# Input of the projection normalised for its later tiles, sample states read before their outer product is added

## The chip, the cores and the metric

The kernel runs on one core of a Trainium2 chip. The metric is the device time of one execution in microseconds (us). A core has TensorE (PE), VectorE (DVE), ScalarE (ACT), GpSimd (POOL) and SyncE (SP, which issues DMAs); each works through its own instructions strictly in order, and they wait for one another by semaphores.

## What is computed

Two layers of a hybrid decoder, on 256 prompt tokens and 8 samples side by side (264 columns). Cut to what matters here:

```
def decoder_layer(x, ...):
    x = x + 0.5 * swiglu(rmsnorm(x, norm_ffn1), ffn1_w_in, ffn1_w_out)
    h = rmsnorm(x, norm_mix)
    proj = h @ w_in
    p_rwkv, p_sc, p_ssm = jnp.split(proj, [RWKV_PROJ, RWKV_PROJ + SC_PROJ], axis=-1)
    ...                                   # three mixers, then w_out, then a second swiglu

rwkv7_mix:       xs = proj + (prev - proj) * mu          # prev: proj shifted by one token
short_conv_mix:  b_gate, c_gate, xt = jnp.split(proj, 3, axis=-1)
                 conv, new_buf = causal_depthwise_conv(c_gate * xt, buf, conv_w)
                 return rmsnorm(b_gate * conv, norm_g), new_buf
mamba2_mix, for a sample (one step):
                 h = h0 * exp(dt * A) + B (outer) (x * dt)
                 y = sum_n(C * h) + D * x
```

## The kernel before

A layer is a front stage and a back stage (`front_stage`, `back_stages`, called through `mix_stages`). The change lies in the front stage alone. There the first feed-forward runs (68 weight tiles), then the combined projection `h @ w_in`, 51 tiles of 128 output columns; tile n = 0 is the tail, 1 to 8 are xbc, 9 and 10 rwkv, 11 to 14 z, 15 to 18 x, 19 to 22 c, 23 to 26 b, 27 to 50 rwkv.

Each tile is 8 x 3 matmuls (`Stream.product`, L232 to L234): the fp32 weights are split into hi and lo, and so is the input. ScalarE makes hi (L209), VectorE or for some tiles GpSimd makes lo (L216). GpSimd makes lo for tiles 0, 2, 14, 16, 18, 20, 22, 24, 44 and 46. The product goes to one of three PSUM banks. The input of the projection is `x * gain` without the factor 1/rms: `norm2` makes `h_hi` and `h_lo` while the feed-forward ends, and the 1/rms (`rs`) is multiplied onto each product when VectorE evicts it (L1153 for rwkv tiles, L1159 for the others). TensorE may begin tile n when tile n-3 has been evicted.

For a rwkv tile VectorE evicts into `front_prev`; ScalarE then writes `mix.xs` (L1122) and `last` (L1124); VectorE adds the shifted part (`shift`, L1132).

Around the tiles, each engine has a side program (`side`) cut by `yield slot`: when the engine has come to tile n it runs the parts with slot <= n. The order of the work is thus written out by hand. VectorE, for tile n: evict(n), shift of tile n-1, lo of tile n+3, side steps. ScalarE, for tile n: side steps, hi of tile n+4, reads of tile n. The side programs hold the rest of the mixers: the conv and its taps (L781), dt and the cumulated sums, the segments (L1233, L1235, L1237) for which TensorE broadcasts rows (L1443, slots 13, 15, 17, 19), the scores (L1253), the state of the prompt (L1484), and the samples. For a sample chunk m of 4: ScalarE decays the state `hst` (L1047, slots 25 and 26) and writes the outer product of B and x*dt (L1059, slots 27, 29, 32, 34); VectorE adds it (L1167), multiplies by C (L1173), reduces (L1177) and adds D*x (L1179). From slot 39 on come the lora gates (TensorE L1520, ScalarE `gates`), the norm of the keys (L1091 to L1097) and the bonus (L1538).

Of the kernel before, what the change touches and what calls it, by code (L numbers as in the profile page):

```python
# [803 lines left out]
def front_stage(nc, env, mix, layer, d):  # L804
# [12 lines left out]
    with Stage(nc, f"front{layer}") as st:  # L817
# [21 lines left out]
        H = len(tiles)  # L839
# [11 lines left out]
        z, bg = at("z", 20832, [P, 4, N]), at("b_gate", 25056, [P, 4, N])  # L851
# [10 lines left out]
        spread, xs_dt = at("spread", 73056, [P, 4, 2 * NS]), at("sample_xdt", 73312, [P, 4, NS])  # L862
# [21 lines left out]
        norm2 = Norm(st, env, "mix", lambda k: env.col("norm_mix", k), A, h_hi, h_lo, rs, xa, ctmp[:, 0])  # L884
# [7 lines left out]
        with nc.Block() as block:  # L892
# [35 lines left out]
            def _(pool):  # L928
# [12 lines left out]
                def side(pool):  # L941
                    yield 42
                    pool.wait_ge(s("state_out"), 64)
                    pool.memset(mix.cum[:, :, :, 0:1], 0.0).then_inc(s("gates_zero"), 1)
# [25 lines left out]
            def _(act):  # L970
# [17 lines left out]

                def side(act):
# [5 lines left out]
                    for slot in range(2, 12):  # L995
                        yield slot
                        if slot < 10:
# [12 lines left out]
                        if slot == 9:  # L1010
                            act.wait_ge(s("tok_ps"), 1)
                            act.activation(tok[:], ps[:, A, 0:32].rearrange("p (a h) -> p a h", a=4), ACT.Copy).then_inc(s("tok_in"), 1)
                    yield 13
                    act.wait_ge(s("btok_ps"), 1)
                    act.activation(btok[:].rearrange("p c g n -> p (c g n)"), ps[:, A, :], ACT.Copy).then_inc(s("btok_done"), 1)
                    yield 14
                    act.wait_ge(s("smp_conv"), 8)
# [21 lines left out]
                    act.activation(spread[:], ps[:, DB, 0:64].rearrange("p (m e) -> p m e", m=4), ACT.Copy).then_inc(s("spread_in"), 1)  # L1039
# [8 lines left out]
                    for m in range(4):  # L1048
                        yield 27 + 2 * m + m // 2
                        if m == 3:  # L1050
                            act.wait_ge(s("sc_gated"), 1)
                            act.wait_ge(s("bc_ps"), 2)
                            act.activation(sq, acc, ACT.Square).then_inc(s("sc_sq"), 1)
# [7 lines left out]
                        if m == 0:  # L1061
# [4 lines left out]
                                          btok[:].rearrange("p c g n -> p (c g) n")).then_inc(s("hfin_stored"), 16)  # L1066
                    yield 37
                    act.wait_ge(s("y_gated"), 1)
                    act.wait_ge(s("sc_ms"), 1)
                    act.activation(sq, ym, ACT.Square).then_inc(s("ssm_sq"), 1)  # L1070
                    for a in range(2):
                        yield 37 + a
                        act.wait_ge(s("kk_done"), a + 1)
                        act.activation(nrm[:, 4 * a:4 * a + 4], mix.kkn[:, 4 * a:4 * a + 4], ACT.Square).then_inc(s("kk_sq"), 1)
                    act.wait_ge(s("new_ps"), 1)
                    act.activation(sc_rows[:], ps[0:18, A, :], ACT.Copy).then_inc(s("rows_done"), 1)
                    for a in range(2):
                        act.activation(cv_rows[:, a * 512:(a + 1) * 512], ps[0:27, DB + a, :], ACT.Copy).then_inc(s("rows_done"), 1)
# [6 lines left out]
                    for p, slot in enumerate((40, 41, 42, 43, 44, 45, 48, 49)):  # L1085
                        yield slot
                        if p == 5:
# [5 lines left out]
                            act.activation(root[:], root[:], ACT.Ln).then_inc(s("norm_ln"), 1)  # L1093
                            act.wait_ge(s("norm_ln"), 3)
                            act.activation(nrm[:], nrm[:], ACT.Exp, scale=-0.5, bias=lnb[:, 0:1]).then_inc(s("norm_inv"), 1)
                            act.activation(sc_root[:], sc_root[:], ACT.Exp, scale=-0.5).then_inc(s("norm_inv"), 1)
                            act.activation(root[:], root[:], ACT.Exp, scale=-0.5).then_inc(s("norm_inv"), 1)  # L1097
                        gates(p)
# [29 lines left out]
            def _(dve):  # L1128
# [14 lines left out]
                def evict(n, kind, m):  # L1143
# [11 lines left out]
                    if kind == "c" and m >= 2:  # L1155
                        dve.wait_ge(s("u_done"), m - 1)
                    dst = {"z": lambda: z[:, m], "xbc": lambda: xbc[:, m, 3:3 + N], "x": lambda: u[:, m, 2:2 + N],
                           "c": lambda: ctmp[:, m % 2], "b": lambda: bg[:, m]}[kind]()
                    dve.tensor_tensor(dst, bank, rs[:], ALU.mult).then_inc(evicted, 1)  # L1159
                    if kind == "c":  # L1160
                        dve.wait_ge(evicted, n + 1)
                        dve.tensor_tensor(u[:, m, 2:2 + N], u[:, m, 2:2 + N], ctmp[:, m % 2], ALU.mult).then_inc(s("u_done"), 1)

                def sample(m):
                    dve.wait_ge(s("outer_in"), NS * (m + 1))
                    dve.wait_ge(s("hst_decayed"), NS * (m + 1))
                    dve.tensor_tensor(hst[:, m], hst[:, m], outer[:], ALU.add).then_inc(s("hst_done"), 1)  # L1167
                    dve.wait_ge(s("hst_done"), m + 1)
# [6 lines left out]
                def sample_out(m):  # L1175
# [1357 lines left out]
```

## Time and profile before

| | |
|---|---|
| median of 3 runs | 1659.33 us (1658.1 to 1665.26) |
| the profiled execution | 1660.52 us, its span 1658.5 us |
| PE busy | 1550.0 us (93%) |
| DVE busy | 1145.6 us (69%) |
| ACT busy | 860.9 us (52%) |
| POOL busy | 264.0 us (16%) |
| projection of layer 0, of layer 1 | about 217 to 430 us, 1033 to 1246 us |

The rows below come from views of the profile. A timeline row is: start in us, duration in us (of the whole row, where it merges several instructions: x2, x3), engine, line, operation, what it writes and reads, shapes, and in brackets the idle time before it and who ended it. Lines (L...) are those of the kernel before. In a window's row the columns are: window, its length, then busy us (and number of instructions) of PE, PEld, DVE, ACT and POOL, then the granted TensorE clock (1.00 is full), the share of the DMA engines and GB/s.

### The profile page before, as it was taken

How to read it: one execution, taken by the hardware profiler on the slowest of the kernel's cores; microseconds unless marked ns; L12 is line 12 of the kernel's file. 1: busy time of each engine (PE TensorE's matmuls, PEld its weight loads, DVE VectorE, ACT ScalarE, POOL GpSimd, SP SyncE). 2: the span in 40 equal slices, each digit the busy share in tenths (PEclk: the TensorE clock that was granted, in tenths of full speed). 3: DMA queues.
4: the chain of work that ended last, by engine and by line, in shares of the span. 5: the costliest groups of instructions: out<-in, count | busy, mean ns of one | idle time of the engine just before them, and what ended most of it. 6: DMA issues, size and time to landing. Idle time of an engine off the chain costs nothing. (4 is left out here: it accounts for less than half of the span.)

```text
span 1658.5 us, 41230 instructions
## 1 busy us (share of the span) xinstructions
PE 1550.0 (93%) x17275; PEld 1471.9 (89%) x17275; DVE 1145.6 (69%) x1832; ACT 860.9 (52%) x1521; POOL 264.0 (16%) x259
## 2 busy tenths in 40 slices
PE   7999999989799899999999999998997989899997
PEld 6999999977688789999999999998775878899997
DVE  6565578795798667665575656978768977676654
ACT  5444465767444555444354444657673445554443
POOL 0000003001455531000000000030014554300000
PEclk9999999999899999999999999999998999999999
DMA  7555557471244445555454655654703453465552
GB/s 232 178 168 176 161 157 211 131 210 52 64 127 119 138 150 171 196 174 187 149 186 153 203 166 175 194 157 131 213 1 104 126 166 111 130 199 181 187 176 71
DMA packets 280649, 256.26 MB, mean 155 GB/s; under 512 B 48054, under 2 KB 268700, under 8 KB 280450
## 3 DMA queue, kind: packets, MB, share of 16 engines
q1 hardware_dynamic: 276698, 252.05, 49.3%
q8 instruction: 138, 2.26, 0.6%
q10 hardware_dynamic: 3768, 1.59, 0.4%
q14 instruction: 45, 0.37, 0.1%
HBM read 242.22 MB, written 11.38 MB: 153 GB/s over the span
## 5 line engine op out<-in xcount | busy, mean ns | idle before, releaser
L209 ACT ACTIVATE front_hi<-front_raw 128x1024 fp32r<-128x1024 f32 (+2 forms) x230 | 238.5, 1039 | 257.2 <-PE ps L234 249.7
L216 DVE TENSOR_TENSOR front_lo<-front_raw,front_hi 128x1024 fp32r<-128x1024 f32 (+1 forms) x210 | 252.2, 1201 | 112.5 <-ACT front_hi L209 111.7
L209 ACT ACTIVATE out_hi<-out_raw 128x1024 fp32r<-128x1024 f32 (+1 forms) x168 | 173.2, 1038 | 216.1 <-PE ps L234 202.5
L216 DVE TENSOR_TENSOR out_lo<-out_raw,out_hi 128x1024 fp32r<-128x1024 f32 (+1 forms) x148 | 183.3, 1239 | 109.9 <-ACT out_hi L209 109.3
L232 PE MATMUL ps<-front_h_hi,front_hi 128*128 128x264 f32 (+1 forms) x816 | 241.2, 296 | 8.6 <-DVE front_lo L216 6.7
L234 PE MATMUL ps<-front_h_hi,front_lo 128*128 128x264 f32 (+1 forms) x816 | 233.0, 286 | 0.0
L233 PE MATMUL ps<-front_h_lo,front_hi 128*128 128x264 f32 (+1 forms) x816 | 232.8, 285 | 0.0
L232 PE MATMUL ps<-ffn_h_hi,out_hi 128*128 128x264 f32 x704 | 200.4, 285 | 0.1
L233 PE MATMUL ps<-ffn_h_lo,out_hi 128*128 128x264 f32 x704 | 199.6, 284 | 0.0
L234 PE MATMUL ps<-ffn_h_hi,out_lo 128*128 128x264 f32 x704 | 199.6, 283 | 0.0
L232 PE MATMUL ps<-in_h_hi,front_hi 128*128 128x264 f32 x688 | 197.3, 287 | 0.0
L233 PE MATMUL ps<-in_h_lo,front_hi 128*128 128x264 f32 x688 | 196.4, 285 | 0.0
L234 PE MATMUL ps<-in_h_hi,front_lo 128*128 128x264 f32 x688 | 196.3, 285 | 0.0
L232 PEld LDWEIGHTS ps<-front_h_hi,front_hi 128*128 128x128 f32 (+1 forms) x816 | 154.0, 189 | 16.8 <-issue 14.2
L233 PEld LDWEIGHTS ps<-front_h_lo,front_hi 128*128 128x128 f32 (+1 forms) x816 | 154.2, 189 | 0.7
L234 PEld LDWEIGHTS ps<-front_h_hi,front_lo 128*128 128x128 f32 (+1 forms) x816 | 153.5, 188 | 0.1
L216 POOL TENSOR_TENSOR front_lo<-front_raw,front_hi 128x1024 fp32r<-128x1024 f32 (+1 forms) x20 | 49.8, 2491 | 540.6 <-ACT front_hi L209 540.6
L232 PEld LDWEIGHTS ps<-ffn_h_hi,out_hi 128*128 128x128 f32 x704 | 132.4, 188 | 0.5 <-ACT ffn_h_hi L283 0.5
L233 PEld LDWEIGHTS ps<-ffn_h_lo,out_hi 128*128 128x128 f32 x704 | 132.4, 188 | 0.1
L234 PEld LDWEIGHTS ps<-ffn_h_hi,out_lo 128*128 128x128 f32 x704 | 132.4, 188 | 0.0
L233 PEld LDWEIGHTS ps<-in_h_lo,front_hi 128*128 128x128 f32 x688 | 131.2, 191 | 0.1
L232 PEld LDWEIGHTS ps<-in_h_hi,front_hi 128*128 128x128 f32 x688 | 131.1, 190 | 0.1
(410 smaller groups left out, 3861.2 us busy)
## 6 DMA issues: line engine op xcount, KB each, us to landing
front_raw<-in_w_in SPq DMA_DIRECT2D x50, 1024.0 KB, 5.4
out_raw<-in_ffn_w_in SPq DMA_DIRECT2D x44, 1024.0 KB, 5.2
front_raw<-in_ffn_w_in SPq DMA_DIRECT2D x40, 1024.0 KB, 5.3
back_sample_rows<-row_scratch SPq DMA_DIRECT2D x160, 128.0 KB, 3.1
out_raw<-in_w_out SPq DMA_DIRECT2D x16, 1024.0 KB, 5.8
front_raw<-in_ffn_w_out SPq DMA_DIRECT2D x16, 896.0 KB, 5.0
out_raw<-in_ffn_w_out SPq DMA_DIRECT2D x16, 896.0 KB, 4.9
front_raw<-in_ffn_w_out SPq DMA_DIRECT2D x8, 1024.0 KB, 5.4
```

The source lines that it names most:

```text
L209: act.activation(self.hi[n % self.RING][:, 0:k, 0:w], self._raw(n), ACT.Copy).then_inc(self.hi_ready, 1)
L216: eng.tensor_tensor(self.lo[n % self.RING][:, 0:k, 0:w], self._raw(n), self.hi[n % self.RING][:, 0:k, 0:w].bitcast(F32), ALU.subtract).the ...
L232: pe.matmul(out, hi[:, j, 0:w], x_hi[:, j], start=start and j == 0, stop=False)
L233: pe.matmul(out, hi[:, j, 0:w], x_lo[:, j], start=False, stop=False)
L234: mm = pe.matmul(out, lo[:, j, 0:w], x_hi[:, j], start=False, stop=stop and j == k - 1)
```

## The change

1. `norm2` now writes its halves into `env.in_hi` and `env.in_lo` (the place of `mix.xs` tiles 0 to 15). They feed tiles 0 to 18. Meanwhile VectorE makes the normalised input `x * gain * rs` (`normed`), ScalarE copies it to `h_hi` (`normed_hi`) and VectorE makes `h_lo` (`normed_lo`), 8 parts of each, in VectorE slots 10 to 18 and ScalarE slots 11 to 17. Tiles from 19 on use these, and their products need no factor.
2. From tile 19 a rwkv tile is no longer evicted by VectorE. ScalarE reads PSUM twice (`mix.xs`, `last`) and VectorE adds the shifted part directly from PSUM (`mix_shifted`), behind its lo of tile n+3. A c tile is multiplied into `u`, a b tile into `acc`. The order of the tiles changes: rwkv 8 to 15 (now n = 23 to 30) come ahead of b (now 31 to 34).
3. The samples are read out of the decayed state: VectorE multiplies `hst` by C and reduces, without the outer product; what that adds to the output is (sum of B*C) times x*dt, computed for all chunks at once (`bc_pair`, one matmul, `smp_own`). GpSimd adds the outer product to `hst` behind the multiplication, one addition for each chunk, in its slot 28; `outer(m)` on ScalarE waits for the addition m-1.
4. Moved: the square of the short conv from slot 34 to 35 of ScalarE, its mean on TensorE from slot 35 to 36, the two last conv parts on VectorE from slots 27 to 31 and 32, the copies of the new rows ahead of the second key square, gates(5) ahead of the logarithms, logarithms and exponentials to slots 46 and 47.

```
-  ("c", SC0 + 512, 0, 4), ("b", SC0, 0, 4), ("rwkv", 8 * P, 8, 8), ("rwkv", 0, 0, 8),
+  ("c", SC0 + 512, 0, 4), ("rwkv", 8 * P, 8, 8), ("b", SC0, 0, 4), ("rwkv", 0, 0, 8),
...
-norm2 = Norm(st, env, "mix", lambda k: env.col("norm_mix", k), A, h_hi, h_lo, rs, xa, ctmp[:, 0])
+norm2 = Norm(st, env, "mix", lambda k: env.col("norm_mix", k), A, env.in_hi, env.in_lo, rs, xa, ctmp[:, 0])
...
     def side(pool):
+        yield 28
+        for m in range(4):
+            pool.wait_ge(s("outer_in"), NS * (m + 1))
+            pool.wait_ge(s("smp_c"), 2 * m + 2)
+            pool.tensor_tensor(hst[:, m], hst[:, m], outer[:], ALU.add).then_inc(s("hst_done"), 1)
...
+    def normed_hi(k):                                    # ScalarE, k = 0, 1, 2, 3, (4, 5), (6, 7) in slots 11, 12, 13, 14, 15, 17
+        act.wait_ge(s("normed"), k + 1)
+        act.activation(h_hi[:, k], ctmp[:, k % 2], ACT.Copy).then_inc(s("normed_hi"), 1)
...
     yield 13
+    normed_hi(2)
     act.wait_ge(s("btok_ps"), 1)
     act.activation(btok[:].rearrange("p c g n -> p (c g n)"), ps[:, A, :], ACT.Copy).then_inc(s("btok_done"), 1)
...
     for m in range(4):                                   # outer(m), slots 27, 29, 32, 34
         if m:
-            act.wait_ge(s("smp_sum"), m)
+            act.wait_ge(s("hst_done"), m)
...
+        if kind == "rwkv" and n >= NORMED:               # ScalarE, NORMED = 19
+            act.wait_ge(ws.used, base + n + 1)
+            bank = ps[:, n % 3, 0:N]
+            act.activation(mix.xs[:, m], bank, ACT.Copy, scale=env.omu[:, m:m + 1]).then_inc(kept, 1)
+            act.activation(last[:, m], bank[:, T - 1:T + NS], ACT.Copy).then_inc(last_in, 1)
         ws.split_hi(act, base + n + 4)
...
+    def mix_shifted(n, m):
+        q, bank = order.index(m), ps[:, n % 3, 0:N]
+        dve.wait_ge(kept, q + 1)
+        dve.wait_ge(last_in, q + 1)
+        dve.scalar_tensor_tensor(out=mix.xs[:, m, 1:T], in0=bank[:, 0:T - 1], scalar=env.col("rwkv_mu", m),
+                                 in1=mix.xs[:, m, 1:T], op0=ALU.mult, op1=ALU.add).then_inc(evicted, 1)
+    def normed(k):
+        if k >= 2:
+            dve.wait_ge(s("normed_lo"), k - 1)
+        dve.scalar_tensor_tensor(out=ctmp[:, k % 2], in0=env.x[:, k], scalar=env.col("norm_mix", k), in1=rs[:],
+                                 op0=ALU.mult, op1=ALU.mult).then_inc(s("normed"), 1)
+    def normed_lo(k):
+        dve.wait_ge(s("normed_hi"), k + 1)
+        dve.tensor_tensor(h_lo[:, k], ctmp[:, k % 2], h_hi[:, k].bitcast(F32), ALU.subtract).then_inc(s("normed_lo"), 1)
...
     def sample(m):
-        dve.wait_ge(s("outer_in"), NS * (m + 1))
         dve.wait_ge(s("hst_decayed"), NS * (m + 1))
-        dve.tensor_tensor(hst[:, m], hst[:, m], outer[:], ALU.add).then_inc(s("hst_done"), 1)
...
-            dve.tensor_tensor(four(outer), four(hst[:, m]), crow, ALU.mult).then_inc(s("smp_c"), 1)
+            dve.tensor_tensor(four(smp_prod), four(hst[:, m]), crow, ALU.mult).then_inc(s("smp_c"), 1)
...
     yield 10
+    normed(0)
     yield 11
+    normed(1)
+    yield 12
+    normed_lo(0)
+    normed(2)
+    yield 13
+    normed_lo(1)
+    normed(3)
     for j in range(4):
         yield 14 + 2 * j
+        if j < 2:
+            for t in (2 + 2 * j, 3 + 2 * j):
+                normed_lo(t)
+                normed(t + 2)
+        if j == 2:
+            normed_lo(6)
+            normed_lo(7)
         ...                                              # the segments
...
-    if n < H:
+    late = kind == "rwkv" and n >= NORMED
+    if n < H and not late:
         evict(n, kind, m)
     ...
     if n + 3 < H and ws.on_dve[base + n + 3]:
         ws.split_lo(dve, base + n + 3)
+    if late:
+        mix_shifted(n, m)
     more.go(n)
```

## Rows read from the trace of the kernel before

**Rows 1.** Busy time by windows, three stretches of layer 0's front stage.
```profile
228.00:256.00 28.00, 26.34 (x216) 25.80 (x215) 27.31 (x52) 21.30 (x35) 0.00 (x0) 1.00 0.65 184
...
300.00:340.00 40.00, 35.80 (x299) 34.81 (x298) 32.09 (x57) 30.44 (x77) 0.00 (x0) 0.99 0.39 118
340.00:372.00 32.00, 28.34 (x199) 26.07 (x199) 29.51 (x50) 20.91 (x44) 0.16 (x1) 0.96 0.83 238
```

**Rows 2.** What TensorE waited for, 215 to 436 us (total us, times, longest).
```profile
PE ps L1538 <- DVE r_k L1334: 4.3, 2, 3.0
PE ps L232 <- DVE front_lo L216: 3.4, 2, 1.7
PE ps L1405 <- DVE outer L1173: 2.5, 1, 2.5
PE ps L1498 <- issue: 1.6, 1, 1.6
PE ps L1507 <- ACT xbc_conv L1070: 1.2, 1, 1.2
PE ps L1520 <- ACT conv_new_rows L1078: 0.8, 1, 0.8
```

**Rows 3.** VectorE in order of time: an `h_lo` of norm2.
```profile
220.28 0.49 DVE L287 SCALAR_TENSOR_TENSOR front_h_lo<-x,cols,front_h_hi 128x264 fp32r<-128x264 f32 x1 [0.18 <-ACT front_h_hi L283]
```

**Rows 4.** VectorE in order of time, layer 0, tiles 8 to 15 and sample 0.
```profile
253.28 1.52 DVE L781 SCALAR_TENSOR_TENSOR xbc_conv<-xbc,cols,xbc_conv 128x256 f32<-128x256 f32 x3
...
256.20 3.72 DVE L781 SCALAR_TENSOR_TENSOR xbc_conv<-xbc,cols,xbc_conv 128x256 f32<-128x256 f32 x3
...
263.87 2.35 DVE L796 TENSOR_TENSOR xbc_conv<-xbc_conv,outer 128x64 f32<-128x64 f32 x1
...
273.09 0.14 DVE L1237 COPY cum_last<-ps 128x1 f32<-128x1 f32 x1
...
326.94 1.28 DVE L1173 TENSOR_TENSOR outer<-sample_state,ps 128x512 f32<-128x512 f32 x2
```

**Rows 5.** TensorE in order of time: row broadcasts of slots 13, 15, 17; a lora product.
```profile
266.17 0.50 PE L1443 MATMUL ps<-cum_rows,pick_row_far 40*128 40x256 f32 x2
...
273.31 0.35 PE L1443 MATMUL ps<-cum_rows,pick_row_far 40*128 40x256 f32 x1
...
280.74 0.38 PE L1443 MATMUL ps<-cum_rows,pick_row_far 40*128 40x256 f32 x1
...
418.81 0.49 PE L1520 MATMUL ps<-xs,w_a 64*128 64x264 f32 x1
```

**Rows 6.** GpSimd in order of time: three of its six subtractions in this stretch.
```profile
257.24 2.40 POOL L216 TENSOR_TENSOR front_lo<-front_raw,front_hi 128x1024 fp32r<-128x1024 f32 x1 [37.09 <-ACT front_hi L209]
263.76 2.38 POOL L216 TENSOR_TENSOR front_lo<-front_raw,front_hi 128x1024 fp32r<-128x1024 f32 x1 [4.13 <-ACT front_hi L209]
271.31 2.75 POOL L216 TENSOR_TENSOR front_lo<-front_raw,front_hi 128x1024 fp32r<-128x1024 f32 x1 [5.17 <-ACT front_hi L209]
```

**Rows 7.** ScalarE in order of time: slot 13, a decay, the first outer product.
```profile
263.59 0.58 ACT L1015 ACTIVATE b_tok<-ps 128x512 f32<-128x512 f32 x1
...
308.24 4.78 ACT L1047 ACTIVATE sample_state<-sample_state,spread 128x128 f32<-128x128 f32 x16
...
319.50 2.09 ACT L1059 ACTIVATE outer<-ps,sample_xdt 128x128 f32<-128x128 f32 x8
```

**Rows 8.** One line's instructions (duration ns min/median/max), whole span.
```profile
L1153 DVE TENSOR_TENSOR front_prev<-ps,front_norm_rs x54: 415/426/435, 228.2 to 1243.4; 128x264 f32<-128x264 f32 x52, 32x264 f32<-32x264 f32 x2
...
L1167 DVE TENSOR_TENSOR sample_state<-sample_state,outer x8: 1207/1217/1220, 325.7 to 1171.2; 128x1024 f32<-128x1024 f32 x8
```

**Rows 9.** ScalarE in order of time: first and last table load around the key norm.
```profile
401.32 1.28 ACT L1091 ACT_TABLE_LOAD   x1
...
409.66 1.28 ACT L976 ACT_TABLE_LOAD   x1
```

**Rows 10.** VectorE in order of time: the last operation of the front stage.
```profile
434.06 0.76 DVE L1359 TENSOR_TENSOR bonus<-xs,ps 128x264 f32<-128x264 f32 x2
```

More of the change, by code:

```diff
@@ L996, in side @@
                         yield slot
+                        if slot == 11:
+                            normed_hi(0)
                         if slot < 10:
@@ L1016, in side @@
                     yield 14
+                    normed_hi(3)
                     act.wait_ge(s("smp_conv"), 8)
@@ L1022, in side @@
                         yield 15 + h // 2 * 2
+                        if h in (0, 2):
+                            normed_hi(4 + h)
+                            normed_hi(5 + h)
                         if h == 0:
@@ L1097, in side @@
                             act.activation(root[:], root[:], ACT.Exp, scale=-0.5).then_inc(s("norm_inv"), 1)
+                        yield slot
                         gates(p)
@@ new lines, in side @@
+                    dve.tensor_tensor(smp_skip[:], xa[:, 0:4, T:N], env.dcol[:].unsqueeze(2).to_broadcast([P, 4, NS]), ALU.mult).then_inc(s("own"), 1)
+                    dve.wait_ge(s("xs_dt"), 1)
+                    for g in range(2):
+                        dve.scalar_tensor_tensor(out=smp_own[:, 2 * g:2 * g + 2], in0=spread[:, 4, NS * g:NS * g + NS].unsqueeze(1).to_broadcast([P, 2, NS]),
+                                                 scalar=float(D), in1=xs_dt[:, 2 * g:2 * g + 2], op0=ALU.mult, op1=ALU.mult).then_inc(s("own"), 1)
@@ new lines, in side @@
+                    dve.wait_ge(s("own"), 3)
+                    dve.tensor_tensor(smp_own[:], smp_own[:], smp_skip[:], ALU.add).then_inc(s("own"), 1)
+                    short_conv(0)
+                    yield 27
+                    short_conv(1)
+                    yield 28
+                    sample(0)
+                    yield 29
+                    scb = env.scb[:].rearrange("p m (b j) -> p m b j", j=2)
+                    conv_sample(dve, s("smp_sc"), acc[:, :, T:N], scn[:, :, 0:NS], [scb[:, :, :, 0], scb[:, :, :, 1], u[:, :, 2 + T:2 + N]],
+                                lambda j: env.col("sc_conv_w", 4 * j, 4))
@@ new lines, in side @@
+                    yield 30
+                    sample(1)
+                    yield 31
+                    short_conv(2)
+                    yield 32
+                    short_conv(3)
+                    dve.wait_ge(s("smp_sc"), 5)
+                    cvb = env.conv[:].rearrange("p m (b j) -> p m b j", j=3)
+                    scw = scn[:, :, 2:18].rearrange("p m (b j) -> p m b j", j=2)
+                    cvw = cvn[:, :, 3:27].rearrange("p m (b j) -> p m b j", j=3)
+                    dve.tensor_copy(scn[:, :, 0:2], u[:, :, T:T + 2]).then_inc(s("new_in"), 1)
@@ new lines, in side @@
+                    yield 33
+                    sample(2)
+                    yield 35
+                    sample(3)
+                    yield 36
+                    dve.wait_ge(s("sc_ms"), 1)
+                    dve.tensor_scalar(sc_root[:], ps[:, EB, 0:N], D / SC, NORM_EPS, ALU.mult, ALU.add).then_inc(s("sc_read"), 1)
+                    dve.wait_ge(s("smp_sum"), 4)
+                    dve.wait_ge(s("own"), 4)
+                    dve.tensor_tensor(ym[:, :, T:N], ym[:, :, T:N], smp_own[:], ALU.add).then_inc(s("smp"), 1)
@@ L1302, in side @@
+                    dve.wait_ge(s("smp"), 1)
                     dve.wait_ge(s("y_done"), 4)
@@ L1390, in _ @@
                         before = tiles[n - 1][1]
-                        shift(before)
+                        if n - 1 < NORMED:
+                            shift(before)
                         if before in (25, 15, 7):
@@ L1463, in side @@
                         mm = head_rows(pe, ps[:, DB, 16 * m:16 * m + 16], ident, m, das[:])
-                    mm.then_inc(s("spread_ps"), 1)
+                    pe.wait_ge(s("bc_pair"), 1)
+                    pe.matmul(ps[:, DB, 64:80], mean, bc_pair[:].rearrange("p g b -> p (g b)"), start=True, stop=True).then_inc(s("spread_ps"), 1)
                     pe.wait_ge(s("bc_lo"), 1)
@@ L1490, in side @@
                     for i in range(ST):
-                        mm = pe.matmul(ps[:, EB, 0:N], mean, sq[:, i], start=i == 0, stop=i == ST - 1)
+                        mm = pe.matmul(ps[:, EB, 0:N], mean, sc_squares[:, i], start=i == 0, stop=i == ST - 1)
                     mm.then_inc(s("sc_ms"), 1)
@@ L1548, in _ @@
                         pe.wait_ge(s("dt_in"), 1)
-                    ws.product(pe, base + n, ps[0:halves[base + n][2], n % 3, 0:N], h_hi, h_lo,
-                               ready=norm2.pe_ready(pe) if n == 0 else None)
+                    hi, lo = (env.in_hi, env.in_lo) if n < NORMED else (h_hi, h_lo)
+                    ws.product(pe, base + n, ps[0:halves[base + n][2], n % 3, 0:N], hi, lo,
+                               ready={0: norm2.pe_ready(pe), NORMED: normed_ready}.get(n))
                     if n == 1:
```

121 lines of the change are left out of this document (54 added, 67 removed).

## The prediction

> **What bounds the kernel now.** I read the busy shares first (the table above): TensorE is the engine that is nearly always busy. A change to VectorE, ScalarE and GpSimd work can therefore only matter where TensorE waits for them. The view by windows cuts layer 0's front stage: from 228 to 256 us VectorE is busy 27.31 of 28.00 us, and between 300 and 372 us TensorE is idle about 8 us of 72 [rows 1]. The list of waits then says for whom it waits [rows 2]: those behind projection tile 22 are 4.3, 1.7 (the longer of the two at L232), 2.5, 1.6, 1.2 and 0.8 us, 12.1 us in a layer. Last I read the queues in order of time, since all are strictly in order. A tile costs TensorE 24 matmuls, some 2.95 us; VectorE splits a weight tile in 1.21 us and evicts in 0.43. Layer 1 shows the same pattern, so each term below counts twice.
>
> **Before the switch (tiles 10 to 19): what is added.** Nothing is removed here. VectorE gets 16 operations on 128x264 (eight `normed`, eight `normed_lo`), in slots 10 to 18 of its side program. The nearest row is the `h_lo` operation of the same shape, 0.49 us, of which about 0.45 is start to start where one waits for the other [rows 3]: 7.2 us. ScalarE gets eight copies of 0.4 us, which cost little by themselves, but each waits for VectorE and holds what stands behind it.
> In the trace VectorE runs without a break from 228 to 273 us, and is late: it still does the conv taps of tile 8 when TensorE is in tile 10, and the last of the segments' rows ends at 273.23 [rows 4]. TensorE's row broadcast, which waits for it, starts at 273.31, and the one of slot 13 at 266.17 [rows 5]. There is no slack to hide anything.
>
> What the rows show beside this is a collision. When GpSimd subtracts at 257.24 us for 2.40 us, three conv taps on VectorE take 3.72 us instead of 1.52; at 263.76 us an addition of 64 elements takes 2.35 us instead of about 0.22 [rows 4, 6]. Both have two inputs in SBUF. The third subtraction, at 271.31, meets the segments, which read PSUM, and costs VectorE nothing, though it takes 2.75 us itself. So a VectorE operation with two SBUF inputs stands still for up to 2.2 us. `normed` and `normed_lo` are such operations, and they stand where GpSimd splits tiles 16, 18, 20 and 22.
>
> The Trainium skill states this as a rule against such a change (page "SBUF — State Buffer", section "Who interferes with whom"): a VectorE instruction with two SBUF inputs contends with a GpSimd instruction that reads SBUF, and the second to issue is blocked until the first has finished. By that rule, the trace agrees (2.2 us each time). With it the sum comes to 1699 us, without it to 1679.
>
> Walking the queues with the old start times:
> - Slot 13. `normed_hi(1)` holds up ScalarE's split of tile 16 until about 266.5, so the stall at 263.87 goes (a gain of 2.1 us) and GpSimd's subtraction falls into VectorE slot 12 instead. VectorE: slot 10 done 264.7, slot 11 done 267.2, split of tile 15 done 268.75, GpSimd to 271.1, then `normed_lo(0)` and `normed(2)` done 272.0. Behind it ScalarE copies `normed_hi(2)` (0.4) and only then `b_tok` (0.58, which ended at 264.17 [rows 7]), for which TensorE's broadcast waits: 273.1 instead of 266.17, **+6.9 us**. Without the collision 270.7, +4.5.
> - Slot 15. Tile 14 runs to 276.4. Then evict and split (1.2) to 277.65, GpSimd to 280.0, four added operations 1.9, segments 1.5: 283.4 instead of 273.31, **+10.1 in all**. Without the collision 279.0, +5.7.
> - Slot 17. From the end of tile 16: evict 0.45, split 1.15, GpSimd 2.35, four operations 1.8, segments 1.5 = 7.25 us. TensorE's own way to that broadcast is 4.05 us (7.43 between the two broadcasts [rows 5], less 0.43 and 2.95). **+3.2**; without the collision +0.85.
> - Slot 19, with two added operations: 6.35 against 4.05, **+2.3**; without it 0.
> Sum: **+15.6 us a layer**, bound below by 6.6 (no collision).
>
> **Tiles 19 to 38.** Here work is removed: a multiplication of 0.43 us for 24 rwkv tiles and 4 c tiles, the gate product of 1.25, and the four additions `hst + outer` of 1.22 us [rows 8], which go to GpSimd. No row shows this addition on GpSimd; the nearest is the subtraction of the same 128x1024, 2.38 to 2.75 us [rows 6], and I take 2.4. It blocks VectorE's next split for about 1.2 us once `tensor_reduce` (one input) is over, so VectorE gains nothing from the move. But two waits are added. First, VectorE's `mix_shifted(n)` waits for ScalarE's two reads of the same tile. The order of tiles puts rwkv at 23 to 30, where ScalarE decays the state, twice 16 copies of 4.78 us, and builds `outer` in 2.1 [rows 7]. Queued behind it on VectorE are the side steps of the slot. Second, `outer(m)` waits for GpSimd's addition m-1, and ScalarE's hi splits and reads are queued behind that. What I get for TensorE:
> - slot 26: VectorE is held until ScalarE has done 16 decays (313.7), `xdt` follows, and the L1484 products wait 1.6;
> - tile 32 waits for `mix_shifted(29)`, behind `outer(1)` 2.1, behind GpSimd 2.4, behind sample(0): 2.4 (was 1.7);
> - slot 32, products of sample(1): 1.0 (was 2.5);
> - slot 36: from the split of tile 36, products 1.28 [rows 4], GpSimd 2.4, `outer(3)` 2.1, hi split 1.0, square 1.07 = 7.85, against tile 36, 2.95: 4.9 (was nothing at L1491);
> - slot 37 waits for `sc_root`, behind sample(3) and a blocked split: 2.3 (was 1.6); slots 38 and 39 stop waiting (was 1.2 and 0.8).
> 12.2 against 7.8 is +4.4. The stretch 340 to 372 has a granted clock of 0.96 instead of 1.00 [rows 1], which is some 3 us at the lower level of 1.2 GHz, worth up to 1.7 us; with TensorE standing elsewhere I take it as gone: **+2.7 us a layer** (-2 to +5). The new column sums (one matmul of 16 columns, five operations of 8 to 32 elements, about 1 us on VectorE) lie in slots 23 and 26 under the wait of slot 26; were that gone they would cost under 1 us.
>
> **Tiles 39 to 50.** The logarithms and exponentials now run in slots 46 and 47. Before they ran from 401.32 to 409.66, 8.3 us, ahead of gates(5) [rows 9], and ended early enough that TensorE's lora product at 418.81 [rows 5] came 13.4 us after tile 45 (end 405.4). After: gates(5) first, then logarithms from 1.65 us behind tile 45's end, reads and split 1.6, exponentials, reads, gates(6) with its table: 15.5. **+2.1**, in spite of the first wait at L1538 (4.3 less 3.0, 1.3 us [rows 2]), half of which goes. Range -1 to +3.
>
> **The end of the stage** is set by VectorE: its last bonus product starts at 434.06 [rows 10], behind an unbroken chain from the last eviction. There `shift(23)` goes (0.4), the wait on ScalarE and the cheaper eviction cancel: **-0.4**. So of TensorE's 3.0 us at L1538 nearly all stays. DMAs: the weight loads queued on SyncE behind `hst_done`, and the copies out of the state, go out up to 4 us later. No wait of TensorE in [rows 2] is for a DMA, so no charge; a missed load would cost what it is late.
>
> **Sum.** 15.6 + 2.7 + 2.1 - 0.4 = 20.0 us a layer, 40.0 in all. The profiled span is 1658.5 (time 1660.52), the median of the three runs 1659.33, 0.8 above the span: 1658.5 + 40.0 + 0.8 = **1699 us**.
>
> **Rivals.**
> - No collision on the added operations: 6.6 early, and 1.2 less later: 9.8 a layer, 1679 us. It would hold if GpSimd's subtractions fell between the added operations. Against it: at slots 16 and 18 both engines are released by the end of the same tile.
> - Faster: the removed VectorE work wins. If all named waits after tile 22 but the last went (1.7, 2.5, 1.6, 1.2, 0.8, 1.3 = 9.1), the dip of the clock (1.7) and 0.4 at the end, 11.2 us a layer are given back. It decides as soon as the early loss stays under that; with `b_tok` not held by `normed_hi(2)` and no collision it would be 4.4 (ten operations ahead of the segments of slot 14), so 6.8 a layer faster, 1646 us. Against it: the ScalarE reads inside VectorE's queue.
> - The two cancel, 1659 us.
> - Worse than forecast: TensorE would idle 6.9 us in slot 13 and 4.4 in slot 15, longer than anywhere in the stage now, and the only reduced clock of these windows, 340 to 372, lies behind the waits of 1.7 and 2.5 us [rows 1, 2]. Two such stretches are 3.4 us a layer: 1706 us.
>
> **Chances.** Forecast 0.50, no collision 0.20, worse by the clock 0.12, faster 0.12, cancelled 0.06. About 0.5% (8 us) is what a measurement of this kernel can tell from no change. So faster 0.12, same 0.06, slower 0.82. The range goes from 1664 (slower cases with a good middle part) to 1712.
>
> **What would show it.** In the profile after: the L1443 broadcasts of slots 13 and 15 with waits of several us; `normed`/`normed_lo` operations of over 2 us beside a GpSimd subtraction; the wait before the mean of the short conv (slot 36); ScalarE idle until the GpSimd addition ends. The early step is wrong if the distance from tile 12 to tile 20 has grown by less than 6 us; the forecast falls if VectorE turns out to reach slot 12 before ScalarE needs it, or if TensorE waits after tile 22 less than 8 us.

## The result, and the profile after

| | before | after |
|---|---|---|
| median | 1661.48 us (1658.1 to 1665.26) | 1718.31 us (1717.77 to 1720.19) |
| span of the profiled execution | 1658.5 us | 1716.2 us |
| mean granted TensorE clock | 0.986 | 0.963 |

The ratio is 1.0343, with a 95% interval of 1.0316 to 1.0371. The change costs 57 us. The forecast was 40 us, 1699 us with a range from 1664 to 1712: the direction was right, the size was too small, and the measured time lies above the range.

The page of the kernel after, its engines and its row of the granted clock in 40 equal slices:

```profile
PE 1582.8 (92%) x17279; PEld 1501.6 (87%) x17279; DVE 1146.8 (67%) x1802; ACT 862.1 (50%) x1537; POOL 279.5 (16%) x267
...
PEclk9999998889899999999999999989898999999999
```

VectorE is busy as long as before (1145.6 us then), so what it saved and what it was given cancel; in what it was given is the time that its operations stand blocked, which counts as busy. TensorE has nearly the same matmuls and is busy 33 us longer (1550.0 us before). More waiting can't do that; a lower clock can: TensorE has two levels, 1.2 and 2.4 GHz, and 1.00 in the profile means 2.4. The view by windows shows it, for the front stage of layer 0 (columns as in [rows 1]; the last row is one tile behind slot 48):

```profile
256.00:285.00 29.00, 19.83 (x129) 18.73 (x128) 23.53 (x43) 10.74 (x19) 8.72 (x3) 0.87 0.57 174
285.00:312.00 27.00, 22.09 (x125) 19.89 (x126) 16.34 (x31) 8.96 (x15) 5.23 (x2) 0.75 0.26 82
312.00:345.00 33.00, 30.86 (x234) 29.40 (x234) 16.81 (x36) 24.81 (x60) 2.62 (x1) 0.86 0.34 105
345.00:368.00 23.00, 22.38 (x180) 21.91 (x180) 19.89 (x34) 14.00 (x39) 4.77 (x2) 0.99 0.35 106
368.00:400.00 32.00, 27.04 (x177) 24.32 (x175) 26.78 (x39) 18.00 (x34) 5.00 (x4) 0.89 0.84 245
400.00:462.00 62.00, 56.01 (x346) 45.78 (x344) 31.25 (x64) 38.87 (x83) 7.36 (x6) 0.94 0.10 31
449.00:455.00 6.00, 6.00 (x27) 5.32 (x27) 2.26 (x3) 2.93 (x6) 2.54 (x4) 0.53 0.00 0
```

A clock of 0.75 means half of the window at 1.2 GHz and half at 2.4, so the time at the lower level is twice what is missing from 1.00: 7.5, 13.5, 9.2, 0.5, 7.0 and 7.4 us, 45 us in these windows. Before, 0.99 and 0.96 between 300 and 372 us give 3.4 us [rows 1]; the rest of the stage, 217 to 300 and 372 to 431 us, shows 1.00.

What TensorE waited for, in the same stage (total us, times, longest; compare [rows 2]):

```profile
PE ps L1522 <- DVE cum_last L1296: 8.1, 3, 4.1
PE ps L1571 <- ACT sc_squares L1087: 5.0, 1, 5.0
PE ps L1618 <- DVE r_k L1409: 3.6, 2, 3.2
...
PE ps L1522 <- ACT b_tok L1033: 2.9, 1, 2.9
PE ps L1600 <- ACT gate L996: 2.6, 1, 2.6
PE ps L1505 <- ACT xbc_conv L1019: 2.2, 1, 2.2
PE ps L1564 <- DVE xdt L1323: 2.1, 1, 2.1
PE ps L232 <- DVE front_lo L216: 1.6, 1, 1.6
PE ps L232 <- DVE front_h_lo L1212: 1.0, 1, 1.0
PE ps L1484 <- DVE sample_prod L1222: 0.6, 1, 0.6
```

These sum to 29.7 us, against 13.8 us in the six rows of [rows 2]. The difference, 16 us, is well short of the 31.5 us by which this stage ends later (its last bonus product starts at 462.20 us, before at 430.74). To find where it comes from, I cut the stage at four TensorE instructions that every variant has: the row broadcasts of slots 13 and 19, the first mean of slot 38 and the last bonus product. Their starts in layer 0, from TensorE's timeline, for all kernels used below:

| kernel | slot 13 | slot 19 | slot 38 | last bonus | 13 to 19 | 19 to 38 | 38 to end |
|---|---|---|---|---|---|---|---|
| before | 266.17 | 288.20 | 363.85 | 430.74 | 22.0 | 75.7 | 66.9 |
| after | 272.62 | 310.45 | 392.47 | 462.20 | 37.8 | 82.0 | 69.7 |
| e1 samples only | 266.35 | 288.33 | 363.33 | 431.00 | 22.0 | 75.0 | 67.7 |
| e2 input only | 271.85 | 309.78 | 391.58 | 461.31 | 37.9 | 81.8 | 69.7 |
| e3 narrow lo | 270.98 | 297.19 | 376.92 | 446.62 | 26.2 | 79.7 | 69.7 |
| e4 filled waits | 272.94 | 307.71 | 388.14 | 457.52 | 34.8 | 80.4 | 69.4 |
| e5 half filled | 272.58 | 304.95 | 384.65 | 451.32 | 32.4 | 79.7 | 66.7 |
| e6 late normed | 266.70 | 288.81 | 368.83 | 435.49 | 22.1 | 80.0 | 66.7 |
| e7 b_tok first | 268.53 | 305.56 | 387.49 | 457.24 | 37.0 | 81.9 | 69.8 |
| e8 no normed | 265.57 | 287.60 | 367.90 | 437.65 | 22.0 | 80.3 | 69.8 |
| e9 square first | 266.47 | 288.56 | 368.77 | 436.97 | 22.1 | 80.2 | 68.2 |
| e10 spread decays | 266.28 | 288.27 | 365.08 | 434.82 | 22.0 | 76.8 | 69.7 |

Of after's 31.5 us, 22.3 have arisen by slot 19, 6.4 come between 19 and 38, and 2.8 behind that.

What happens in slots 12 to 15, engine by engine. TensorE (start, duration, what ended its idle time):

```profile
272.62 0.50 PE L1522 MATMUL ps<-cum_rows,pick_row_far 40*128 40x256 f32 x2 [2.87 <-ACT b_tok L1033]
```

VectorE, GpSimd and ScalarE:

```profile
269.15 2.48 DVE L1207 SCALAR_TENSOR_TENSOR c_gate<-x,cols,front_norm_rs 128x264 f32<-128x264 f32 x1
...
277.80 0.43 DVE L1195 TENSOR_TENSOR z<-ps,front_norm_rs 128x264 f32<-128x264 f32 x1 [4.96 <-PE ps L234]
...
279.28 2.59 DVE L1212 TENSOR_TENSOR front_h_lo<-c_gate,front_h_hi 128x264 fp32r<-128x264 f32 x1
```

```profile
267.58 3.75 POOL L216 TENSOR_TENSOR front_lo<-front_raw,front_hi 128x1024 fp32r<-128x1024 f32 x1 [7.84 <-ACT front_hi L209]
278.99 2.59 POOL L216 TENSOR_TENSOR front_lo<-front_raw,front_hi 128x1024 fp32r<-128x1024 f32 x1 [7.66 <-ACT front_hi L209]
```

```profile
271.66 0.42 ACT L1000 ACTIVATE front_h_hi<-c_gate 128x264 fp32r<-128x264 f32 x1 [4.15 <-DVE c_gate L1207]
271.99 0.58 ACT L1033 ACTIVATE b_tok<-ps 128x512 f32<-128x512 f32 x1
```

To be read from below: TensorE waits for `b_tok`, `b_tok` stands behind `normed_hi(2)`, that waits for VectorE's `normed(2)`, and this takes 2.48 us instead of 0.49 because GpSimd is subtracting until 271.33 (e3 tests this below). Then VectorE in its turn is idle for 4.96 us until TensorE has finished tile 14. The two engines wait for each other by turns, and TensorE's tiles in between run in part at 1.2 GHz.

### The profile page after: what moved, and what is told of

It is laid out like the page before. It is cut to its first block and busy times, and to the rows that moved or that the text cites. A ratio compares the mean times of both kernels' runs of the same rounds, so it can differ in the third digit from the quotient of the medians.

```text
span 1716.2 us, 41248 instructions
## 1 busy us (share of the span) xinstructions
PE 1582.8 (92%) x17279; PEld 1501.6 (87%) x17279; DVE 1146.8 (67%) x1802; ACT 862.1 (50%) x1537; POOL 279.5 (16%) x267
## 5 line engine op out<-in xcount | busy, mean ns | idle before, releaser
L232 PE MATMUL ps<-in_h_hi,front_hi 128*128 128x264 f32 x992 | 291.4, 294 | 4.8 <-DVE front_lo L216 3.3
L233 PE MATMUL ps<-in_h_lo,front_hi 128*128 128x264 f32 x992 | 287.7, 290 | 0.0
L234 PE MATMUL ps<-in_h_hi,front_lo 128*128 128x264 f32 x992 | 287.5, 290 | 0.0
L232 PEld LDWEIGHTS ps<-in_h_hi,front_hi 128*128 128x128 f32 x992 | 192.8, 194 | 8.3 <-issue 7.8
L234 PEld LDWEIGHTS ps<-in_h_hi,front_lo 128*128 128x128 f32 x992 | 191.8, 193 | 0.1
L232 PE MATMUL ps<-front_h_hi,front_hi 128*128 128x264 f32 x512 | 157.7, 308 | 4.9 <-DVE xs L1201 3.0
L233 PE MATMUL ps<-front_h_lo,front_hi 128*128 128x264 f32 x512 | 150.1, 293 | 0.0
L234 PE MATMUL ps<-front_h_hi,front_lo 128*128 128x264 f32 x512 | 150.1, 293 | 0.0
L232 PEld LDWEIGHTS ps<-front_h_hi,front_hi 128*128 128x128 f32 x512 | 102.2, 200 | 10.8 <-issue 3.8
L233 PEld LDWEIGHTS ps<-front_h_lo,front_hi 128*128 128x128 f32 x512 | 102.2, 200 | 0.7
```

The lines of the kernel that those rows point to most:

```text
L232: pe.matmul(out, hi[:, j, 0:w], x_hi[:, j], start=start and j == 0, stop=False)
L233: pe.matmul(out, hi[:, j, 0:w], x_lo[:, j], start=False, stop=False)
L234: mm = pe.matmul(out, lo[:, j, 0:w], x_hi[:, j], start=False, stop=stop and j == k - 1)
```

## Experiments

| kernel | median us | ratio to before | interval |
|---|---|---|---|
| e1 samples only | 1658.8 | 0.9994 | 0.9982 to 1.0007 |
| e2 input only | 1719.97 | 1.0353 | 1.0333 to 1.0373 |
| e3 narrow lo | 1688.77 | 1.0168 | 1.0150 to 1.0185 |
| e4 filled waits | 1714.11 | 1.0326 | 1.0295 to 1.0356 |
| e5 half filled | 1703.52 | 1.0264 | 1.0245 to 1.0284 |
| e6 late normed | 1673.0 | 1.0076 | 1.0055 to 1.0098 |
| e7 b_tok first | 1706.59 | 1.0281 | 1.0263 to 1.0300 |
| e8 no normed | 1670.79 | 1.0073 | 1.0054 to 1.0092 |
| e9 square first | 1668.51 | 1.0064 | 1.0049 to 1.0078 |
| e10 spread decays | 1662.76 | 1.0031 | 1.0018 to 1.0044 |

The median of the kernel before beside them was 1659.65 (e1 to e4), 1659.92 (e5 to e8) and 1658.93 us (e9, e10).

**Which part carries the loss: e1 and e2.** e1 is before with part 3 of the change alone. Its main lines (`...` stands for the sum that makes up for the outer product, which is added once at the end, and for its buffers):

```
 GpSimd, slot 28:
+    pool.tensor_tensor(hst[:, m], hst[:, m], outer[:], ALU.add)        # for each m
 ScalarE, outer(m):
-    act.wait_ge(s("smp_sum"), m)
+    act.wait_ge(s("hst_done"), m)
 VectorE, sample(m):
-    dve.tensor_tensor(hst[:, m], hst[:, m], outer[:], ALU.add)
-    dve.tensor_tensor(four(outer), four(hst[:, m]), crow, ALU.mult)
+    dve.tensor_tensor(four(smp_prod), four(hst[:, m]), crow, ALU.mult)
 ...
```

> The kernel before with part 3 of the change alone: samples read out of the decayed state, own share added at the end, GpSimd adds the outer product, outer(m) waits for addition m-1. Order of tiles, eviction and norm as before. Theory (the loss is the normalised input ahead of VectorE's just-in-time steps in slots 12 to 19, and the lower TensorE clock that its waits bring): this part is worth little, 0 to +4 us a layer, so 1661 to 1669 us, ratio 1.00 to 1.005. Rival (the GpSimd additions and the wait of outer(m) for them carry the loss): most of the 57 us, ratio over 1.02.

e2 is after with the same part turned back.

> The kernel after with the samples as before (VectorE adds the outer product, outer(m) waits for the reduction m-1, no own share). Theory: nearly all of the loss stays, 1704 to 1718 us; the wait of slot 36 (4.96 us) shrinks, as outer(3) no longer stands behind two operations on two engines. Rival (samples carry it): under 1680 us.

Measured: 0.9994 and 1.0353. By the medians, 1658.8 and 1720.0 us, both lie 2 us outside the expected ranges, on the side away from the rival. The samples' part moves nothing by itself, and taking it out of after gives nothing back. In e2 the wait of slot 36 falls from 5.0 to 2.9 us, as expected, but waits of 2.0 us for `sc_root` (slot 37) and 1.9 us for the products (slot 32) stand in its place, and the stretch from slot 19 to 38 is as long as in after (81.8 and 82.0 us). The loss is in the input's part and what came with it.

**The place of the normed operations: e6 and e8.** e8 leaves them out, with the factor that they apply:

```
-norm2 = Norm(..., env.in_hi, env.in_lo, rs, xa, ctmp[:, 0])
+norm2 = Norm(..., h_hi, h_lo, rs, xa, ctmp[:, 0])
-hi, lo = (env.in_hi, env.in_lo) if n < NORMED else (h_hi, h_lo)
+hi, lo = h_hi, h_lo
-normed(k), normed_hi(k), normed_lo(k)                                  # all of them
```

> The kernel after without the normalised input: norm2 writes h_hi and h_lo as before and these feed all tiles; the sixteen normed operations and their copies on ScalarE are left out, and with them the factor 1/rms of tiles 19 to 50 (left out of the computation). All other parts of the change stay. Theory: slots 12 to 19 run as before, and what is left is the forecast's 4.4 us a layer of the other parts: 1664 to 1672 us. Rival (the later tiles, ScalarE's reads of PSUM and the new order, carry a good part): over 1680 us; if these parts save what VectorE no longer does: under 1655 us.

e6 keeps them, later and one pair at a time:

```
-H, NORMED = len(tiles), 19
+H, NORMED = len(tiles), 23
 VectorE:
-    slots 10 to 18, ahead of each slot's own steps
+    slot 14 + 2j behind the segments:  normed_lo(2j - 1), normed(2j)
+    slot 15 + 2j behind the scores:    normed_lo(2j), normed(2j + 1)
+    slot 22:                           normed_lo(7)
 ScalarE:
+    normed_hi(2j) in slot 15 + 2j behind the exponentials, normed_hi(2j + 1) in slot 16 + 2j
 c tiles:
+    dve.tensor_tensor(u[:, m, 2:2 + N], u[:, m, 2:2 + N], rs[:], ALU.mult)
```

> The kernel after with the sixteen normed operations one at a time behind the timed steps of slots 14 to 22 on VectorE (one normed and one normed_lo in each slot, behind the segments or the scores), normed_hi one slot behind on ScalarE behind its exponentials, and tiles from 23 on (not 19) fed by them; the c tiles (19 to 22) get their factor rs in a further operation on u. Same added work and four more operations. Theory (not the work but its place ahead of the rows, b_tok and the segments costs): the +24 us a layer before slot 19 go but for some 2 us a layer, 1668 to 1682 us. Rival (VectorE has no room in this stretch at all): over 1700 us.

Measured: 1670.8 us without them, 1673.0 us with all of them late, 1718.3 us as in after. By the ratios the sixteen operations, with their copies on ScalarE, cost 45 us where the change puts them. Some slots later, with four operations more, they cost 0.5 us by the ratios and 2.2 us by the medians; the intervals of e6 and e8 overlap, so this can't be told from nothing. Both expectations held. Slots 13 to 19 take 22.1 us in e6, as before the change. GpSimd's subtractions meet them there too:

```profile
273.78 1.18 DVE L1204 SCALAR_TENSOR_TENSOR c_gate<-x,cols,front_norm_rs 128x264 f32<-128x264 f32 x1
...
280.47 1.21 DVE L1209 TENSOR_TENSOR front_h_lo<-c_gate,front_h_hi 128x264 fp32r<-128x264 f32 x1
```

They take 1.2 us instead of 0.5, but nothing is queued behind them on which TensorE waits.

**The collision: e3.**

```
-ws.split_lo(pool, base + n)
+ws.split_lo(pool, base + n, 8 if n in (16, 18, 20, 22) else None)      # columns taken
```

> The kernel after; GpSimd's subtraction for tiles 16, 18, 20 and 22 takes 8 of 128 columns (the rest of those lo halves is left out). It takes the collision with VectorE's two-input operations away. By the forecast's working the collision is 9.0 us of the 15.6 in slots 12 to 19: with the waits shorter there is also less of the lower clock, so theory: 9 to 13 us a layer faster, 1692 to 1700 us. Rival (the added operations themselves and ScalarE's queue make the waits, the collision is hidden): under 3 us a layer, 1712 to 1718 us.

Measured: 1688.8 us, 29.5 us less than after, 15 us a layer. That is more than expected, and it includes what the shorter waits give back in clock. `normed(2)` is the plainest row, 2.48 us in after:

```profile
269.49 0.49 DVE L1208 SCALAR_TENSOR_TENSOR c_gate<-x,cols,front_norm_rs 128x264 f32<-128x264 f32 x1
```

The broadcast of slot 19 starts at 297.19 us, 9.0 us later than before the change; the forecast's working without the collision gave 6.6, and 15.6 with it. Of the 13.3 us by which it is earlier than in after, that working explains 9.0; the rest I put down to the clock, which this run doesn't separate.

**ScalarE's order: e7.**

```
 ScalarE, slot 11: tap and SiLU
-    behind normed_hi(0)
+    ahead of normed_hi(0)
 ScalarE, slot 13: b_tok
-    behind normed_hi(2)
+    ahead of normed_hi(2)
```

> The kernel after with two pieces of ScalarE's order exchanged: in slot 11 the tap and SiLU ahead of normed_hi(0), in slot 13 b_tok ahead of normed_hi(2). By the forecast's step for slot 13 TensorE waits for b_tok because it stands behind normed_hi(2). Theory: waits of slots 12 and 13 (2.2 and 2.9 us) shrink to under 1 us each, but the segments of slot 15 are behind the same operations of VectorE, so what is won in slot 13 is waited for in slot 15: 0 to 3 us a layer, 1712 to 1718 us. Rival (ScalarE's queue carries the early loss): 5 us a layer or more, under 1709 us.

Measured: 1706.6 us, by the ratios 10 us and by the medians 12 us less than after. My expectation missed, and the time is in the range of the rival: ScalarE's queue is worth 5 to 6 us a layer of the loss. The wait of slot 12 falls from 2.2 to 0.4 us and that of `b_tok` from 2.9 to 1.7. The wait of slot 15 grows from 4.1 to 5.2 us, as expected, but the lead is kept: slot 13 is 4.1 us earlier than in after, slot 19 4.9 and slot 38 5.0. VectorE's slot 14 can't begin before TensorE has finished tile 14, so what TensorE wins in slot 13 moves VectorE too. The gains of e3, e5 and e7 can't be added up (29, 13 and 10 us by the ratios, more than the 45 us of all sixteen operations): each edit also shortens waits that the others act on.

**The clock: e4 and e5.** Both put matmuls whose results nobody reads ahead of eight waits of TensorE:

```
+def fill(n, count):
+    ...
+    if n > 40:
+        pe.wait_ge(evicted, n - 1)
+    for _ in range(count):
+        pe.matmul(ps[:, ..., 384:512], x[:, 1, 0:P], x[:, 0, 0:128], start=True, stop=True)
...
+fill(12, 28)                            # e5: 14
 pe.wait_ge(s("xa_done"), 8)
...
+fill(13 + 2 * j, (38, 58, 44, 0, 0)[j]) # e5: 19, 29, 22
...                                      # slots 26, 36, 48, 50 in the same way
```

> The kernel after with additional matmuls of 128 columns, whose results nobody reads, ahead of TensorE's waits in slots 12, 13, 15, 17, 26, 36, 48 and 50 (28, 38, 58, 44, 28, 70, 36 and 44 of them, 1.7 to 4.2 us at the full clock, each less than the wait it stands ahead of). Nothing waits less by it; TensorE only isn't idle there. Theory (idle TensorE is followed by stretches at 1.2 GHz, and those are the part that the forecast missed, some 10 us a layer): granted clock back to 0.98 or more, 8 to 11 us a layer faster, 1696 to 1703 us. Rival (the missing part is other waits, the clock costs little because TensorE would otherwise wait there anyway): within 3 us of 1718, or slower.

Measured: 1714.1 us, with a clock of 0.989. I had sized the matmuls wrongly, as TensorE's timeline of e4 shows:

```profile
268.65 4.35 PE L1493 MATMUL ps<-in_h_hi 128*128 128x128 f32 x38
272.94 0.50 PE L1531 MATMUL ps<-cum_rows,pick_row_far 40*128 40x256 f32 x2
```

38 of them take 4.35 us where TensorE waited 2.87. They outlast the waits, so that e4 gives back clock and pays for it with later starts; it falls between the two expected ranges, and its interval overlaps that of after. It says nothing about what the clock is worth. e5 has half as many.

> As e4_filled_waits with half the additional matmuls (14, 19, 29, 22, 14, 35, 18 and 22). In e4 each took 0.114 us, as long as one of 264 columns (38 of them 4.35 us, 58 of them 6.59), so they outlasted the waits that they stood ahead of (2.9 and 4.1 us) and e4 is no fair test of the clock. Now they take 1.6, 2.2, 3.3, 2.5, 1.6, 4.0, 2.1 and 2.5 us at the full clock, each a little less than its wait. Theory (lower clock is the missing part): clock 0.985 or more and 8 to 11 us a layer less than after, 1696 to 1703 us. Rival (TensorE merely reaches the next wait earlier and waits longer there): the clock is back, but the time falls by less than 6 us in all, 1712 to 1718 us, with the waits longer by what the tiles are shorter.

Measured: 1703.5 us, 13 us less than after by the ratios and 14.8 by the medians; the profiled span is 16.9 us shorter (1699.3 us, clock 0.982). The windows of e5 that answer to those of after:

```profile
256.00:285.00 29.00, 24.94 (x192) 24.32 (x190) 23.52 (x43) 10.73 (x19) 8.76 (x3) 0.94 0.56 173
285.00:305.00 20.00, 17.46 (x139) 15.81 (x138) 15.19 (x29) 7.64 (x14) 5.21 (x2) 1.00 0.27 83
305.00:384.00 79.00, 73.76 (x592) 70.96 (x593) 57.91 (x100) 50.23 (x119) 12.36 (x6) 0.98 0.53 163
384.00:451.00 67.00, 65.51 (x435) 54.53 (x433) 38.72 (x73) 46.62 (x97) 7.85 (x7) 1.00 0.17 50
```

Some 7 us at 1.2 GHz instead of 45, and layer 0's last bonus product starts 10.9 us earlier than in after. In layer 1 it is 7.2 us (from one last bonus product to the other: 815.6 us before, 843.3 after, 836.1 in e5). The time is 0.5 us above the range that I had expected and the clock a little under 0.985; by the medians it is 7.4 us a layer instead of 8 to 11, and far from the rival. Nothing was taken off any engine's path: the difference is that TensorE had work instead of idling. The rival is right for one stretch: the broadcasts of slots 13 and 15 start at the same time as in after (272.58 and 284.77 us), since VectorE sets them; the lower clock costs nothing there. From slot 17 on it does.

**What is left in e6: e9 and e10.** e6 still needs 80.0 us from slot 19 to 38 (75.7 before) and waits 5.0 us for the square. e9 puts the square ahead of the last outer product on ScalarE:

```
 for m in range(4):
+    if m == 3:
+        yield 35
+        act.wait_ge(evicted, 35)
+        act.activation(sc_squares[:], acc, ACT.Square)
     yield 27 + 2 * m + m // 2
     ...                                 # outer(m)
```

> e6_late_normed with the square of the short conv ahead of outer(3) on ScalarE (outer(3) moves to slot 35 behind it). In e6 TensorE still waits 5.0 us in slot 36, and the stretch from the row broadcast of slot 19 to the mean of slot 38 takes 80.0 us against 75.7 before. By the forecast's step this wait comes from outer(3) standing behind GpSimd's addition 2, with the square queued behind it. Theory: the wait goes, 4 to 5 us a layer less, 1662 to 1666 us. Rival (the square would wait for the b tiles' eviction or the next step is late by as much): less than 1 us a layer, 1671 to 1675 us.

Measured: 1668.5 us. The interval (1.0049 to 1.0078) overlaps that of e6. The wait did go, but another stands behind it:

```profile
PE ps L1568 <- DVE sc_root L1362: 3.8, 1, 3.8
...
PE ps L1561 <- ACT sc_squares L1069: 0.7, 1, 0.7
```

From slot 19 to 38 it is 80.2 us, as in e6. The expectation (1662 to 1666 us) was wrong, and the time is under the rival's 1671 to 1675 too, but the rival had the mechanism: the next step is late by nearly as much. TensorE now waits in slot 37 for `sc_root`, which is late on VectorE. e10 spreads the decays over four slots of ScalarE:

```
-for m in range(4): yield 25 + m // 2; decay(m)
+decay(0) in slot 25, decay(1) in 26, decay(2) in 28, decay(3) in 30
```

> e9 with the decays on ScalarE one chunk at a time in slots 25, 26, 28 and 30 instead of two each in 25 and 26, so that ScalarE's reads of the rwkv tiles, for which VectorE's mix_shifted waits, stand behind 2.4 us of decays and not 4.8. Theory: TensorE's wait for xdt in slot 26 (2.1 us) and the one before tile 32 go, 2 to 3 us a layer less than e9, 1656 to 1662 us, no slower than before. Rival (outer(1) and outer(2) now come later and hold the row broadcast of slot 32 and sample(2)): same as e9 or slower.

Measured: 1662.8 us, ratio 1.0031 (1.0018 to 1.0044). That is 0.8 us above the expected range, and the kernel is slower than before by a little that is clear of the noise, where I had expected it no slower. The wait for `xdt` in slot 26 is no longer in the list, the one before tile 32 is still 1.1 us (1.2 in e9), the wait for `sc_root` is 3.3 us, and slots 19 to 38 take 76.8 us. Of what holds `sc_root`, 1.2 us is the collision again, here with GpSimd's additions (VectorE, then GpSimd; the same split takes 1.22 us elsewhere); no run takes this collision away:

```profile
355.93 2.42 DVE L216 TENSOR_TENSOR front_lo<-front_raw,front_hi 128x1024 fp32r<-128x1024 f32 x1
```

```profile
354.90 2.37 POOL L949 TENSOR_TENSOR sample_state<-sample_state,outer 128x1024 f32<-128x1024 f32 x1 [4.65 <-DVE sample_prod L1226]
```

With the three edits 52 of the 57 us are given back (by the ratios, 1.0343 less 1.0031), but no variant is faster than the kernel before beyond its interval; e1 comes out even with it.

## Why the prediction was right in direction and too small in size

Taken step by step in layer 0, as the broadcasts' delay against before. The column "TensorE kept busy" is e5, in which the clock is nearly undisturbed.

| step | forecast | TensorE kept busy (e5) | after |
|---|---|---|---|
| up to slot 13 | 6.9 | 6.4 | 6.5 |
| up to slot 15 | 10.1 | 11.5 | 11.5 |
| up to slot 17 | 13.3 | 14.7 | 17.4 |
| up to slot 19 | 15.6 | 16.8 | 22.3 |
| from 19 to 38 | 2.7 | 4.0 | 6.4 |
| from 38 to the end | 1.7 | -0.2 | 2.8 |
| a layer | 20.0 | 20.6 | 31.5 |

**The early slots** were right in mechanism, and e3, e6 and e8 show each piece of it: it is the place of the operations that costs, and by the forecast's own split three fifths of it through the collision. The walk through the queues came within 1.5 us at each broadcast as long as the clock is left out. One thing in it was wrong: it knew no wait in slot 12 (2.17 us, for a SiLU behind `normed_hi(0)`), and it had the stall of slot 12 meet `normed_lo(0)`, where it met `normed(2)`. That ScalarE's order in slots 11 and 13 costs something was foreseen for slot 13 alone; e7 puts a price on both together, 10 to 12 us in all.

**Tiles 19 to 38.** The waits named were right where the clock lets them be seen. In after, slot 26 waits 2.1 us (forecast 1.6), slot 32 0.6 (1.0), slot 36 5.0 (4.9); tile 32 (2.4) and slot 37 (2.3) don't wait in layer 0. In e5 both do, 2.7 and 1.7 us:

```profile
PE ps L232 <- DVE xs L1201: 2.7, 1, 2.7
...
PE ps L1590 <- DVE sc_root L1372: 1.7, 1, 1.7
```

Slow tiles of TensorE had covered them in after: from 340 to 358 us, ahead of tile 32, its clock is 0.85. In e7 it is 1.00 in the 18 us ahead of tile 32 (335 to 353), and the wait of 2.7 us stands there without any added matmuls. A wait that is missing from the list may be hidden behind a slower engine. The step that failed here is the one that took the old dip of the clock as gone (1.7 us of gain), in a stretch that now has 17 us of it.

**Tiles 39 to 50.** The forecast of 1.7 us (2.1 for the logarithms, less 0.4) was wrong: with the clock left alone the stretch takes 66.7 us, 66.9 before. The late gates do bring a wait of 2.6 us in slot 48, but the stretch as a whole is no longer than before. What after loses there is time at the lower level behind this wait:

```profile
446.98 0.49 PE L1600 MATMUL ps<-xs,w_a 64*128 64x264 f32 x1 [2.62 <-ACT gate L996]
```

Tile 49 behind this wait takes 5.2 us (449.79 to 455.00). In e6 the same wait of 2.62 us precedes it in layer 0, and the tile takes 3.0 us (425.28 to 428.29, clock 1.00). With the lora products ahead of it (2.8 us from 446.98, in e6 1.9 from 423.35) that is all of the 3.1 us between the two kernels in this stretch. In layer 1 of e6 it waits 2.61 us and the clock does fall. That is also why the last column of the table of starts holds 66.7 in some kernels and 69.7 in others, and a profile may stand a few us off its kernel's median (that of e6 took 1668.2 us, that of e10 1669.2). The windows of e6 behind the wait of layer 0 and of layer 1:

```profile
425.00:431.00 6.00, 6.00 (x45) 5.59 (x44) 4.49 (x7) 3.69 (x9) 2.81 (x4) 1.00 0.00 0
1245.00:1250.00 5.00, 5.00 (x27) 4.87 (x26) 0.63 (x2) 1.35 (x5) 2.62 (x4) 0.66 0.00 0
```

**The clock** is the term that was mis-sized, and it is nearly the whole miss. The sum had it as a gain of 1.7 us a layer, and a rival of 12% had two stretches of it, 3.4 us; what e5 gives back is 10.9 us in layer 0 and 7.2 in layer 1, on top of a sum that was otherwise right to 1 us a layer. That agreement is in part luck: in e5 the three parts of the stage miss by 1.2, 1.3 and -1.9 us and cancel to 0.6. In all e5 still stands 4.5 us above the forecast's 1699. The reason for taking it small was that before had only one dip, of 0.96 [rows 1]. But before has no wait of TensorE over 0.5 us between 256 and 315 us, where slots 12 to 19 lie, and after has one of 2 to 4 us in each of slots 12, 13, 15 and 17.

The Trainium skill, page "TensorE: Matmul & The Clock Gate", section "HAM oscillation — how this bites in real kernels", describes a matmul loop broken by waits that drops to the lower clock again at each of them; the windows of after agree that the clock falls behind waits, but not at each of them (e6, layer 0). It prices the loss at half of the time spent at the lower clock. By that the 38 us that e5 takes away in layer 0 would be worth 19 us, an estimate from that page. e5 gives back 10.9. One reason is shown: up to slot 15 that time costs nothing, as VectorE sets the broadcasts; how the rest divides, no run shows.

The other rivals: "no collision" is refuted by the rows at 269.15 and 279.28 and by e3. "Faster" and "cancelled" fall with e8: even with no normed operation at all the other parts cost 11 us, near the 8.8 that the forecast has for them.

## What to carry to other kernels

Work that fills an engine's idle time has to go into the slots where the engine is idle, behind its timed steps: the same operations cost 45 us ahead of them and some slots later no more than about 2 us, which can't be told from nothing. Before costing a wait of the busiest engine at its own length, add what its clock loses behind it when waits follow one another; the cheapest test is to give the engine useless work in the wait, sized below it. And where two engines share a resource, look at what is queued behind the operation that is blocked, not at the operation.

## What was unexpected of the hardware

- A matmul of this type on 128 columns takes as long as one on 264: 0.114 us each (38 in 4.35 us), against 0.12 us from start to start in a tile's 24. I had sized e4 at half of that. Each of the 38 comes with a weight load (4.33 us for all), so the trace doesn't tell which of the two sets the pace.
- The collision blocks both ways. In after GpSimd's subtraction at 267.58 takes 3.75 us where the one at 257.36 took 2.39: it starts 0.02 us behind VectorE's split (267.56) and ends at 271.33, which is why `normed(2)` stands until 271.6. In e3 the same place has 1.72 us for 8 columns, against 0.55 at 275.84.
- The same wait of TensorE, 2.6 us with the same work around it, was followed by time at 1.2 GHz in one layer of one execution and not in the other (e6). The length of a wait alone doesn't tell whether it costs clock.
- In layer 0, 38 us less at 1.2 GHz were worth 10.9 us, about 0.3 us for each, where a tile that runs at the lower level in a stretch where TensorE is the bound loses 2.2 of its 5.2 us.
